# Embedding gates in pieces of eight blocks, side splits moved or halved, the final norm's weights on ScalarE

## The reference

```python
for i in range(2):
    u = rmsnorm(h, norm_mix_g[i])
    m = rglru_mixer(u, ...) if i % 2 == 0 else ssd_mixer(u, ...)
    h = h + m
    u = rmsnorm(h, norm_ffn_g[i])
    h = h + (silu(u @ ffn_w_gate[i]) * (u @ ffn_w_up[i])) @ ffn_w_down[i]
    gate = sigmoid(rmsnorm(h, norm_ple_g[i]) @ ple_w_gate[i])     # 2048 x 2048
    h = h + gate * (p[i] @ ple_w_proj[i])                         # 256 x 2048
return rmsnorm(h, final_norm_g)
```

## Time and profile before

| what | value |
|---|---|
| runs | 2737.05, 2737.88, 2750.62 us, median 2737.88 |
| profiled execution | 2750.44 us, its span 2748.7 us |
| busy in the span | TensorE 98%, VectorE 74%, ScalarE 49%, GpSimd 13% |
| mean granted clock | 0.994 of full |
| DMA | 504.54 MB, mean 184 GB/s |

### The profile page before, as it was taken

How to read it: one execution, slowest core, us unless ns; L and a number is a source line. 1 busy time by engine, 2 the same in 40 slices (tenths; PEclk the granted TensorE clock), 3 DMA queues, 4 the chain that set the end, 5 groups by cost and what they waited for, 6 DMA issues and landing times.

```text
span 2748.7 us, 50850 instructions
## 1 busy us (share of the span) xinstructions
PE 2701.8 (98%) x17807; PEld 2463.1 (90%) x17807; DVE 2031.9 (74%) x2818; ACT 1339.4 (49%) x1818; POOL 364.9 (13%) x410
## 2 busy tenths in 40 slices
PE   7999999999999999999999999999999999999997
PEld 7999788888888888999998999988888888888897
DVE  8888876655666677888886688888667557667776
ACT  5676344444444444446664466643444444444443
POOL 3333200000000011200001000021000000001122
PEclk9999999999999999999999999999999999999999
DMA  5555565656655555555555655545665565665654
GB/s 196 184 176 174 171 192 186 188 169 185 197 184 186 195 184 168 173 195 186 183 186 177 205 183 184 185 156 184 190 192 186 178 207 185 192 190 176 189 179 147
DMA packets 162727, 504.54 MB, mean 184 GB/s; under 512 B 18048, under 2 KB 24512, under 8 KB 161472
## 3 DMA queue, kind: packets, MB, share of 16 engines
q1 hardware_dynamic: 162544, 503.14, 57.8%
q10 hardware_dynamic: 80, 0.07, 0.0%
HBM read 500.97 MB, written 2.16 MB: 183 GB/s over the span
## 4 chain that ended last, share of the span: by engine, by line
PE 90%; DVE 8%; DMA 1%; issue 0%; ACT 0%; SPq 0%; DVEq 0%; POOL 0%; ACTq 0%
PE bank L398 39%; PE bank L400 20%; PE bank L381 10%; PE bank L383 10%; PE bank L382 10%; DVE wlo L852 3%; DVE R L885 1%; DVE h L1095 1%; DVE R L883 1%; DVE h L1094 0%; PE bank L571 0%; ACT whi L607 0%; PE bank L562 0%; DMA wraw<-in_A 0%; DVE rinvh L893 0%
## 5 line engine op out<-in xcount | busy, mean ns | idle before, releaser
L398 PE MATMUL bank<-R,whi 128*128 128x512 f32 x4992 | 1752.0, 396 | 7.9 <-DVE R L885 4.9
L852 DVE TENSOR_TENSOR wlo<-wraw,whi 128x1024 fp32r<-128x1024 f32 (+3 forms) x1056 | 1198.5, 1145 | 572.4 <-ACT whi L607 570.3
L607 ACT ACTIVATE whi<-wraw 128x1024 fp32r<-128x1024 f32 (+3 forms) x1056 | 992.9, 947 | 974.3 <-PE bank L400 744.6
L400 PE MATMUL bank<-R,wlo 128*128 128x256 f32 x4992 | 1399.9, 280 | 0.0
L398 PEld LDWEIGHTS bank<-R,whi 128*128 128x128 f32 x4992 | 937.0, 188 | 231.1 <-DVE R L885 5.5
L400 PEld LDWEIGHTS bank<-R,wlo 128*128 128x128 f32 x4992 | 943.8, 189 | 0.2
L381 PE MATMUL bank<-R,whi 128*128 128x256 f32 x2368 | 683.4, 289 | 20.9 <-DVE R L909 13.0
L383 PE MATMUL bank<-R,wlo 128*128 128x256 f32 x2368 | 672.8, 284 | 0.0
L382 PE MATMUL bank<-R,whi 128*128 128x256 f32 x2368 | 672.7, 284 | 0.0
L381 PEld LDWEIGHTS bank<-R,whi 128*128 128x128 f32 x2368 | 456.5, 193 | 30.0 <-issue 15.5
L382 PEld LDWEIGHTS bank<-R,whi 128*128 128x128 f32 x2368 | 457.3, 193 | 2.2 <-issue 1.9
(11 more groups left out here) (166 smaller groups left out, 1294.8 us busy)
## 6 DMA issues: line engine op xcount, KB each, us to landing
wraw<-in_F SPq DMA_DIRECT2D x352, 512.0 KB, 3.9
wraw<-in_B SPq DMA_DIRECT2D x224, 512.0 KB, 3.5
wraw<-in_A SPq DMA_DIRECT2D x96, 512.0 KB, 4.1
wraw<-in_F SPq DMA_DIRECT2D x128, 384.0 KB, 3.1
wraw<-in_F SPq DMA_DIRECT2D x128, 320.0 KB, 3.2
wraw<-in_PL SPq DMA_DIRECT2D x64, 320.0 KB, 3.1
wraw<-in_PL SPq DMA_DIRECT2D x64, 256.0 KB, 2.8
arena<-cs_rows SPq DMA_DIRECT2D x8, 1024.0 KB, 6.7
```

The lines of the kernel that those rows point to most:

```text
L398: nc.tensor.matmul(dst.rearrange("p (s t) -> p s t", s=2), whi[:, q % RING, cols], src[:, :, k, :], start=first, stop=False)
L400: mm = nc.tensor.matmul(dst[:, 0:SEQ], wlo[:, q % RING, cols], src[:, 0, k, :], start=False, stop=last)
L607: nc.scalar.activation(whi[:, slot, 0:w * BLOCK], wraw[:, slot, 0:w * BLOCK], ACT.Copy).then_inc(w_hi, 1)
L852: V.tensor_tensor(wlo[:, slot, 0:w * BLOCK], wraw[:, slot, 0:w * BLOCK], whi[:, slot, 0:w * BLOCK].bitcast(F32), ALU.subtract).then_inc(w_ ...
```

## The change

The embedding phase PL gets pieces of 8, 8, 8, 8 and 4 blocks, and all its eight pairs of tiles are written out in one iteration of 40 steps, on every engine. Its gate, tanh and `h` steps move to fitting steps; the stats product comes after piece 0. The splits of the embedding move into step 1 of the last iteration of the F2 before it; the two parts of the split of the time steps' weights move to steps 8 and 13 (ScalarE) and 9 and 14 (VectorE) of the written-out phase.

In A2 and in B2's second half, the high part of a side tile (the multiply by the gain) is made by ScalarE one step after the fold, for the first seven of the eight tiles of a pass; VectorE makes the low part of the tile of the step before (`u_low`) and the last tile as it did.

In PL of layer 1 ScalarE multiplies each finished tile of `h` by its final gain into `gained_h`, a part of the arena that nothing else uses then. At the end five VectorE products (of 4, 4, 4, 2 and 2 tiles) multiply it by the scale, and five stores follow. The last norm leaves out the half of its scale.

```diff
+LAST = ((0, 4), (4, 4), (8, 4), (12, 2), (14, 2))
-        t.append(("PL", layer, 0, 8, [5, 5, 4, 4] * 2, 4))
+        t.append(("PL", layer, 0, 8, [8, 8, 8, 8, 4], 4))
...
+            if ph["name"] == "PL":
+                ph.update(iters=1, widths=ph["widths"] * 8, groups=ph["groups"] * 8)
...
-            for m in range(KT):
-                sp.wait_ge(out_ready, m + 1)
-                sp.dma_start(out[:, m, :], h[:, m, :]).then_inc(out_done[m % 2], 16)
-            for s in out_done:
-                sp.wait_ge(s, 16 * KT // 2)
+                if ph["iters"] > 1:
+                    with sp.Fori(1, ph["iters"]) as it:
+                        body(it, False)
+            for c, (m, n) in enumerate(LAST):
+                sp.wait_ge(out_ready, c + 1)
+                sp.dma_start(out[:, m:m + n, :], h[:, m:m + n, :]).then_inc(out_done, 16)
+            sp.wait_ge(out_done, 16 * len(LAST))
...
-                        if norm is not None and first and q == (3 if norm == 0 else 1):
+                        if norm is not None and first and q == (3 if norm == 0 else 0 if name == "PL" else 1):
...
+                def gain(m):
+                    act.wait_ge(h_done, KT + m + 1)
+                    nc.scalar.activation(gained_h[:, m, :], h[:, m, :], ACT.Copy,
+                                         scale=gains[:, 6 * KT + m:6 * KT + m + 1]).then_inc(gained, 1)
+
+                def gate_tanh(m):
+                    act.wait_ge(bank_free, gate0 + 2 * m + 1)
+                    nc.scalar.activation(swi_t[:, m % 2, :], swi_g[:, m % 2, :], ACT.Tanh).then_inc(ple_t, 1)
...
-                        if name == "PL" and ph["layer"] == 0 and first and q == 5:
-                            split_dt_weights()
+                        if name == "PL" and ph["layer"] == 0 and q in (8, 13):
+                            split_dt_weights(q // 13)
+                        if name == "F2" and ph["half"] == 1 and last and q == 1:
+                            split_p_high()
...
+                        if name in PAIRED and next_norm(ph) is not None and q > 8:
+                            j = q - 9
+                            k, m = next_norm(ph), it * 8 + j
+                            act.wait_ge(bank_free, it * 8 + ph["group0"] + 4 + j + 1)
+                            nc.scalar.activation(R[next_u(k)][:, 0, m, :], h[:, m, :], ACT.Copy,
+                                                 scale=gains[:, k * KT + m:k * KT + m + 1]).then_inc(uh_done, 1)
...
+                        if name == "PL":
+                            if q % 5 == 0 and q:
+                                gate_tanh(q // 5 * 2 - 1)
+                            if q % 5 == 2:
+                                gate_tanh(q // 5 * 2)
+                            if q == n - 1:
+                                gate_tanh(KT - 1)
+                            if ph["layer"] == 1 and q % 5 in (1, 3) and q > 1:
+                                gain((q - 3) // 5 * 2 + (q % 5 == 1))
...
+                u_low(norm, m, count, buf)
+
+            def u_low(norm, m, count, buf):
+
+                g = gains[:, at(m + norm * KT)]
+                dst = R[buf]
+                def tile(x):
+                    return x.rearrange("p a t -> p (a t)")
                 dve.wait_ge(uh_done, count)
                 V.scalar_tensor_tensor(out=tile(dst[:, 1, at(m), :]), in0=tile(h[:, at(m), :]), scalar=g,
                                        in1=tile(dst[:, 0, at(m), :]).bitcast(F32), op0=ALU.mult, op1=ALU.subtract
@@ -892,6 +931,8 @@
...
+                if k == 6:
+                    return
...
+                def gated_tile(m, p):
+                    g0, j = ph["group0"] + 4, m % 2
+                    done = m + ph["layer"] * KT + 1
+                    dve.wait_ge(w_used, p + 1)
+                    dve.wait_ge(ple_t, done)
+                    V.scalar_tensor_tensor(out=swi_g[:, j, :], in0=swi_t[:, j, :], scalar=1.0,
+                                           in1=bank[BANKS4[2 * j + 1]][:, 0:SEQ], op0=ALU.add, op1=ALU.mult
+                                           ).then_inc(bank_free, 1)
+                    dve.wait_ge(bank_free, g0 + 2 * m + 2)
+                    V.scalar_tensor_tensor(out=h[:, m, :], in0=swi_g[:, j, :], scalar=0.5, in1=h[:, m, :],
+                                           op0=ALU.mult, op1=ALU.add).then_inc(h_done, 1)
+                    if ph["layer"] == 0:
+                        dve.wait_ge(h_done, done)
+                        u_split(3, m, m + 2 * KT + 1, next_u(3))
...
-                                    dve.wait_ge(bank_free, g0 + j + 1)
-                                    u_split(next_norm(ph), m, m + (next_norm(ph) - 1) * KT + 1, next_u(next_norm(ph)))
+                                    k = next_norm(ph)
+                                    if name in PAIRED and j > 0:
+                                        u_low(k, m - 1, m + (k - 1) * KT, next_u(k))
+                                    if name not in PAIRED or j == 7:
+                                        dve.wait_ge(bank_free, g0 + j + 1)
+                                        u_split(k, m, m + (k - 1) * KT + 1, next_u(k))
...
+                            if q % 5 == 0 and q:
+                                gated_tile(q // 5 * 2 - 1, p - 1)
+                            if q % 5 in (1, 4):
...
+                            if q % 5 == 2:
+                                gated_tile(q // 5 * 2, p)
+                            if q == n - 1:
+                                gated_tile(KT - 1, p)
...
-            for m in range(KT):
-                V.scalar_tensor_tensor(out=h[:, m, :], in0=h[:, m, :], scalar=gains[:, 6 * KT + m:6 * KT + m + 1],
-                                       in1=rinv[:], op0=ALU.mult, op1=ALU.mult).then_inc(out_ready, 1)
+            dve.wait_ge(gained, KT)
+            for m, n in LAST:
+                V.tensor_tensor(h[:, m:m + n, :], gained_h[:, m:m + n, :],
+                                rinv[:].rearrange("p (a t) -> p a t", a=1).broadcast_to([P, n, SEQ]), ALU.mult
+                                ).then_inc(out_ready, 1)
```

More of the change, by code:

```diff
@@ L258, in steps @@
                     body(it, False)
-            chain.begin(ph["iters"] - 2, per)
-            body(ph["iters"] - 1, False)
-            chain.close(ph["iters"] - 1)
+            if ph["iters"] > 1:
+                chain.begin(ph["iters"] - 2, per)
+                body(ph["iters"] - 1, False)
+                chain.close(ph["iters"] - 1)
         def width_of(index, ph, q, last):
@@ L323, in body @@
                         row = it + src0
+                        if ph["name"] == "PL":
+                            row, at0 = q // 5, P * PIECE * BLOCK * (q % 5)
                         if ph["name"] in PAIRED:
@@ L630, in _, with split_p_high @@
                 if name == "PL":
-                    src = R[u_buf[("PL", ph["layer"])]]
+                    gate0 = ph["group0"] + 4
+                def split_p_high():
                     act.wait_ge(p_in, 16 * (ph["layer"] + 1))
-                    nc.scalar.activation(src[:, 0, 20:22, :], praw.rearrange("p (k t) -> p k t", k=2), ACT.Copy
-                                         ).then_inc(p_hi, 1)
+                    nc.scalar.activation(R[u_buf[("PL", ph["layer"])]][:, 0, 20:22, :],
+                                         praw.rearrange("p (k t) -> p k t", k=2), ACT.Copy).then_inc(p_hi, 1)
+                def gain(m):
[5 more added lines that the diff above has]
+                    nc.scalar.activation(swi_t[:, m % 2, :], swi_g[:, m % 2, :], ACT.Tanh).then_inc(ple_t, 1)
                 def decay_steps(q):
@@ L645, in decay_steps, with split_dt_weights @@
                                              scale=-1.0).then_inc(dec_exp, 1)
-                def split_dt_weights():
+                def split_dt_weights(part):
                     act.wait_ge(g_landed, 16 * (LRU_HEADS + 1))
[L649 to L652, removed]
+                    r, lo = ((1, 0), (0, 1024))[part]
+                    nc.scalar.activation(R[r][:, 0, 16:20, :], graw[:, lo:lo + 1024].rearrange("p (k t) -> p k t", k=4),
+                                         ACT.Copy).then_inc(g_hi, 1)
                 def gates(head):
@@ L839, in _ @@
                 steps(act, ph, body, own, 4 if name == "B1" else 0)
+            gain(KT - 1)
             norm(6)
@@ L955, in _, with split_dt_weights @@
                 own.close(1)
[L957 to L963, removed]
+                def split_dt_weights(part):
+                    dve.wait_ge(g_hi, LRU_HEADS + 1 + part)
+                    r, at0 = ((1, 0), (0, 1024))[part]
+                    V.tensor_tensor(R[r][:, 1, 16:20, :], graw[:, at0:at0 + 1024].rearrange("p (k t) -> p k t", k=4),
+                                    R[r][:, 0, 16:20, :].bitcast(F32), ALU.subtract).then_inc(g_lo, 1)
                 def decay_steps(q):
@@ L1045, in body @@
                             norm(norm_of(ph))
```

(25 more changed lines are left out.)

19 lines of the change are left out of this document (7 added, 12 removed).

## The result

The changed kernel took 2711.99 us, the median of four executions (2709.55 to 2712.96), against 2737.47 (2736.55 to 2750.62): ratio 0.9877, interval 0.9841 to 0.9914. The direction was right and the size was not: 25.5 us were gained where 16.3 were worked out.

What follows compares the result with a forecast made beforehand. TensorE, busy 2701.8 of 2748.7 us, was taken as the bound, with its waits and matmul pitch. Gains of 9.8 + 4.8 + 1.7 = 16.3 us from the 2737.9 median gave 2721.6 us, range 2714 to 2740.

Steps and rivals of the forecast that it cites:

- Part 1: Side splits of A2 and B2, multiply moved to ScalarE: 9.8 us gained, bounds 1.4 and 12.2.
- I take 3.3, near the plain subtraction: VectorE's step per piece in A2 and B2 falls from 3.63 to 3.3 us; plain subtraction gives 3.24.
- my lower bound of 2.9: Shortest VectorE step in A2 and B2, 2.9 us, if the low half gets in front of GpSimd's add.
- The six waits: TensorE's waits for low halves in A2 and B2, 4.6 us; five would go, for 4.3 us.
- The pitch of each stage is drawn anew: Feed-forward stages: changed restarts of TensorE redraw each stage's pitch; a long one costs 13.8 us.
- Part 2: Embedding stage of layer 0, border to B1 and added stats waits: 4.8 us gained, bounds 3.0 and 6.5.
- The decay steps of B1 (another dip) don't change: B1's decay steps, with another clock dip, stay as they are; no gain counted.
- Part 3: The tail, five products and five stores: 1.7 us gained, bounds 0.5 and 2.7.
- The term for the transfer: Tail stores: 2.1 MB at 332 GB/s takes 6.3 us, so the end comes 1.1 us earlier.
- the lock that keeps the step at 3.63: Rival, A2 and B2: GpSimd's port order leaves some 1.4 us of gain there, 2730.0 us; chance 0.09.
- the gain of nil at the end: Rival, tail: the last large store lands later, no gain, 2723.3 us; counted within the forecast's 0.52.
- One long stage and two: Rivals, feed-forward stages at the long pitch: one, 2735.4 us, chance 0.28; both, 2749.2 us, chance 0.07.

Runs made afterwards that it cites:

- part 2 alone: The changed kernel with the old side splits and the old end, leaving only the embedding stage in pieces of eight: 2743.6 us, ratio 0.9964.

## Why the prediction missed

**Part 1: the step failed at "I take 3.3, near the plain subtraction".** Priced at 9.8, it gave 8.3 us in layer 0 (22.04 less the pitch) and 7.0 in layer 1, 15.2 together. I saw the contention in the `lo` of 1.76 us, but not the same 0.26 us in L885's 0.74, and in the value that I took GpSimd keeps its place in the order; the other order stood only in the bound. In the change the low part runs before GpSimd's square and not beside it, and the next low half comes before the add. The step is 2.74 us, under my lower bound of 2.9, which was too high by my own rows too: 3.24 less the 0.55 on the low half is 2.69. The Trainium skill (SBUF — State Buffer, section Who interferes with whom) says that the two engines exclude each other and that the issue order decides which of them waits. The measurement agrees in direction: the loss moved from VectorE (L885's 0.74 to 0.48) to GpSimd (0.81 to 1.60). The lengths fit a full wait of the later one only roughly: before, the low half was 0.54 us longer where 0.69 of the add were left.

With that step nothing is late. The six waits gave 4.7 us (4.3 forecast). At F1's start 8.6 us went for both layers, by the starts of the same blocks in both traces (5.5 forecast: 4.0 for the gaps and 1.5 for half of the clock dips). The last 1.9 us had no term: they are blocks at the long pitch, most of them 123 in A2's and 117 in B2's last pass, 6.7 ns each; since A2 can run long without a wait, its share of 0.8 us is not a sure gain.

**The pitch: read rightly in the profile, judged wrongly for the change.** That two pitches exist, that one stage costs 13.8 us and that the median had none agree with the three clusters of the 45 executions. "The pitch of each stage is drawn anew" failed. In 40 of 40 executions without a wait in A2 or B2 both feed-forward stages were short, whatever pitch A2 had. I had this evidence, all undisturbed entries short, and still gave 0.35 to long stages after the change. That held up the top of the range; it did not cause the miss at its lower end. The gain against a typical execution of before is larger than the given median said: 24 of 45 executions of the kernel before take 14 us more than its lowest cluster.

**Part 2:** 4.8 forecast, 6.1 measured (6.41 - 0.34) in the first profile, 5.2 in part 2 alone and in the second profile of the changed kernel (370.95 and 104.39). The border left a wait of 1.4 us for 2.41, and the stats waits cost 0.67 us each for 0.6. The two embedding stages lie 1.6 us apart, not within 1 us as I had asked for; the border is most of that. "The decay steps of B1 (another dip) don't change" was wrong for the first profile. These stretches, behind the same wait of 1.8 us, are of the kernel before and of the one after:

```profile
1223.00:1226.40 3.40, 3.40 (x18) 0.50 0.93 305
```
```profile
1195.10:1198.50 3.40, 3.40 (x31) 1.00 0.87 295
```

The wait stayed and the dip did not come. In the changed kernel run again it came: the clock was at half from 1196.9 for 3.4 us. So this is no gain of the change; the dip comes with the same wait or it does not. Without it the first profile is 1.4 us shorter there, and 0.6 longer by the short wait in B1: that is the 0.8 between 6.1 and 5.2.

**Part 3:** 1.7 forecast, 2.3 measured, 2.1 by undoing it. The products took 4.70 us as worked out. From the first product to the end of the span it is 8.2 us for 8.7. The term for the transfer was mis-sized: from the stretch with rows of 1 KB I had 332 GB/s at full share, but stores of mostly 4 KB rows moved 408. These are VectorE and SyncE at the end and the stores in flight, of the kernel after:

```profile
2702.86 4.70 DVE L1301 TENSOR_TENSOR h<-arena,rinv 128x1024 f32<-128x1024 f32 x5 [0.48 <-ACT rinv L624]
```
```profile
2704.11 4.24 SPq L381 DMA_DIRECT2D out_hT<-h  x5
```
```profile
2704.00:2706.00 2.00, 0.00 (x0) 0.00 (x0) 2.00 (x3) 0.00 (x0) 0.00 (x0) 0.50 0.53 213
2706.00:2708.00 2.00, 0.00 (x0) 0.00 (x0) 1.56 (x3) 0.00 (x0) 0.00 (x0) 0.50 1.01 408
```

At 408 GB/s the share is 1.01. I take it that the transfer is now the limit in the second half; eight parts of two tiles (380 GB/s at 1.03) gained only 0.3.

Of the rivals, the lock that keeps the step at 3.63 is out, and so is the gain of nil at the end. One long stage and two did not occur.

Still open: why TensorE, at full clock and never idle, has two pitches for the same instructions, and what in a restart chooses. Open too is why all 19 stages that TensorE entered without a wait became or stayed short. The shares differ, about 0.38 of stages long in the kernel before (34 of 90, by the clusters) and one of six with one wait; a dozen executions do not tell whether the number of waits makes that.

## What to carry to other kernels

Before pricing an instruction by the time that it takes off an engine, look at what runs beside it on the other user of its port: here 0.39 us of work taken away brought 0.89 us a step, because it also changed who came first. Compare stretches with the same instruction count and no idle time; if they differ, a wait elsewhere may have a price that its own length doesn't show, and taking out the last such wait can be worth more than the sum of the waits, as it was here in most executions. And give the kernel before enough executions to see its clusters before a median of three is taken for its time.

## What the hardware showed that was not expected

- Two pitches of one instruction stream: 353.3 and 346.7 ns per block of two matmuls (512 and 256 columns), held over 2064 blocks at granted clock 1.00; 13.8 us a stage. A2 had either in executions of one kernel (348 or 341 matmuls in 60 us).
- Where VectorE and GpSimd both read SBUF, the one that starts second was the longer one: the same add on GpSimd took 0.81 or 1.60 us, the same product on VectorE 1.22 or 1.76.
- After each of the two 2.45 us waits of TensorE at F1 the clock was at half for 3.4 us in the kernel before; after the same 1.8 us wait in B1 it was so in some executions and not in others.
- Stores of 1 KB rows moved 269 GB/s at a share of 0.81, of mostly 4 KB rows 408 at 1.01, of 2 KB rows 380 at 1.03.
